# Prompt attention with two output banks in PSUM used in turn, and two in place of three banks for transposed probabilities

## The reference

```python
def block(q0):                       # 128 queries
    s = einsum('bqghd,bngd->bqghn', qc, ck) * SCALE      # compressed keys
    p_c = masked_softmax(s, ...)
    o_c = einsum('bqghn,bngd->bqghd', p_c, cv)
    ...
    p_s = masked_softmax(s, kpos <= pos)                 # selected blocks of 64 keys
    o_s = einsum('bqghm,bqgmd->bqghd', p_s, v_s)
    ...
    p_w = masked_softmax(s, wm)                          # window of 512 keys
    o_w = einsum('bqghk,bkgd->bqghd', p_w, v_w)
    return g[..., 0:1] * o_c + g[..., 1:2] * o_s + g[..., 2:3] * o_w
```

## Time and profile before

| | us |
|---|---|
| median of 3 runs | 2075.46 |
| lowest, highest | 2073.04, 2078.39 |
| profiled execution, device time | 2073.38 |
| its span, first to last instruction | 2071.7 |
| prompt attention, first scores' preparation to last drain | 446.4 to 807.4 |
| mean granted clock of TensorE | 0.927 |

### The profile page before, as it was taken

How to read it: one execution, slowest core, us unless ns; L and a number is a source line. 1 busy time by engine, 2 the same in 40 slices (tenths; PEclk the granted TensorE clock), 3 DMA queues, 4 the chain that set the end, 5 groups by cost and what they waited for, 6 DMA issues and landing times. The chain is left out here.

```text
span 2071.7 us, 26793 instructions
## 1 busy us (share of the span) xinstructions
PE 1848.6 (89%) x9832; PEld 1586.5 (77%) x9832; DVE 1039.9 (50%) x1928; ACT 837.6 (40%) x1702; POOL 185.4 (9%) x334
## 2 busy tenths in 40 slices
PE   5996995979888997949969996999999999999997
PEld 4896873668677775738847885999998999989996
DVE  3532244857677875445434343544445544464444
ACT  4310222536566665232126442433334433343443
POOL 0001202114333321010000000000000000000000
PEclk8998796977889998969979998999999999999998
DMA  5513604400000002133012110333334333344431
GB/s 183 199 45 74 152 4 132 124 9 1 1 1 1 1 1 76 56 136 124 1 61 93 51 61 11 133 122 123 134 139 161 124 122 121 121 159 156 153 130 66
DMA packets 110649, 184.56 MB, mean 89 GB/s; under 512 B 19248, under 2 KB 80112, under 8 KB 110471
## 3 DMA queue, kind: packets, MB, share of 16 engines
q1 hardware_dynamic: 90495, 156.32, 22.0%
q0 software_dynamic: 8080, 25.26, 3.7%
q10 hardware_dynamic: 11968, 1.58, 0.6%
HBM read 174.64 MB, written 12.73 MB: 90 GB/s over the span
## 5 line engine op out<-in xcount | busy, mean ns | idle before, releaser
L2406 DVE TENSOR_TENSOR mlp_dn_lo<-top_w_out_raw,mlp_dn_hi 128x1024 fp32r<-128x1024 f32 x96 | 117.6, 1225 | 299.5 <-ACT mlp_dn_hi L2329 299.5
L2246 PE MATMUL mlp_psU<-mlp_xT_hi,mlp_up_hi 128*128 128x384 f32 (+1 forms) x768 | 253.9, 331 | 5.3 <-DVE mlp_up_lo L2400 5.3
L2246 PE MATMUL mlp_psU<-mlp_xT_lo,mlp_up_hi 128*128 128x384 f32 (+1 forms) x768 | 252.1, 328 | 0.0
L2246 PE MATMUL mlp_psU<-mlp_xT_hi,mlp_up_lo 128*128 128x384 f32 (+1 forms) x768 | 252.0, 328 | 0.0
L2329 ACT CAST mlp_dn_hi<-top_w_out_raw 128x1024 fp32r<-128x1024 f32 x96 | 100.6, 1048 | 267.4 <-PE mlp_acc L2268 187.4
L2268 PE MATMUL mlp_acc<-mlp_dn_hi,mlp_h_hi 128*128 128x512 f32 x512 | 199.4, 389 | 0.0
L2268 PE MATMUL mlp_acc<-mlp_dn_hi,mlp_h_lo 128*128 128x512 f32 x512 | 199.2, 389 | 0.0
L2268 PE MATMUL mlp_acc<-mlp_dn_lo,mlp_h_hi 128*128 128x512 f32 x512 | 199.2, 389 | 0.0
L2246 PEld LDWEIGHTS mlp_psU<-mlp_xT_hi,mlp_up_hi 128*128 128x128 f32 x768 | 145.0, 189 | 9.4 <-issue 3.3
L2246 PEld LDWEIGHTS mlp_psU<-mlp_xT_lo,mlp_up_hi 128*128 128x128 f32 x768 | 145.1, 189 | 3.1
L2246 PEld LDWEIGHTS mlp_psU<-mlp_xT_hi,mlp_up_lo 128*128 128x128 f32 x768 | 145.0, 189 | 0.0
(11 more groups left out here) (399 smaller groups left out, 3974.0 us busy)
## 6 DMA issues: line engine op xcount, KB each, us to landing
top_w_out_raw<-in_w_up SPq DMA_DIRECT2D x48, 1024.0 KB
top_w_out_raw<-in_w_down SPq DMA_DIRECT2D x48, 1024.0 KB
cross_mem<-in_cache_mem_kv SPq DMA_DIRECT2D x8, 1024.0 KB, 4.9
qkv_w_raw<-in_w_in SPq DMA_DIRECT2D x8, 652.0 KB, 5.9
mem_w_raw<-in_w_mkv SPq DMA_DIRECT2D x8, 512.0 KB, 4.9
cmp_raw<-in_cache_cmp_kv SPq DMA_DIRECT2D x32, 128.0 KB
cmp_raw<-in_cache_cmp_kv POOLq DMA_DIRECT2D x32, 128.0 KB, 6.6
smp_sel<-in_cache_sel_kv SPq DMA_DIRECT2D x32, 128.0 KB
```

Source lines behind the costliest of these rows:

```text
L2246: m = nc.tensor.matmul(psU[n % 2][:, 0:w], a[:, u % 2, c, :], b[:, g % 2, c, 0:w], start=(c == 0 and n_pass == 0), stop=(c == KC - 1 and n ...
L2406: nc.vector.tensor_tensor(dn_lo[:, u % 2], dn_raw[:, k, a, :], dn_hi[:, u % 2].bitcast(F32), ALU.subtract).then_inc(s_dl, 1)
```

## The change

The output of a unit gets two banks, taken in turn by u % 2; the first product of unit u waits for the drain of unit u-2 in place of u-1. The transposed probabilities (and the prep steps' transposes) get two banks in place of three, so a transposing step waits for the drain of the one two before it in place of three. The number of banks stays eight. No instruction is added or removed.

```diff
-        psT = [ph.ps(f"psT{k}", [P, 4, P]) for k in range(3)]
-        psO = ph.ps("psO", [P, 4, P])
+        psT = [ph.ps(f"psT{k}", [P, 4, P]) for k in range(2)]
+        psO = [ph.ps(f"psO{k}", [P, 4, P]) for k in range(2)]
...
                     pe.wait_ge(s_th, n + 1)
-                    if arg == 0 and u:
-                        pe.wait_ge(s_od, u)
-                    out = psO[:, :, :].rearrange("p a b -> p (a b)")
+                    if arg == 0 and u >= 2:
+                        pe.wait_ge(s_od, u - 1)
+                    out = psO[u % 2][:, :, :].rearrange("p a b -> p (a b)")
...
-                        halves = psO[:, :, :].rearrange("p (m e) t -> p e m t", e=2)
+                        halves = psO[u % 2][:, :, :].rearrange("p (m e) t -> p e m t", e=2)
```

## The result

| | before | after |
|---|---|---|
| median of the runs, us | 2075.19 (4 runs) | 2094.57 (4 runs) |
| lowest, highest | 2073.04, 2078.39 | 2091.33, 2097.20 |
| profiled execution, device time | 2073.38 | 2095.39 |
| its span | 2071.7 | 2093.7 |
| end of the last drain (start and length of the last L1431) | 807.4 | 829.4 |

The ratio of the times is 1.0091 [1.0075, 1.0108]: the change costs 19.4 us on the medians, where the sum said 22.5.

A forecast was written before the change was run, and what follows sets the result against it. No engine is full; an order of waits sets the attention stage's time, and the kernel follows it. Passes 11 to 14, 6 to 10, 1 to 5, 15 and 16: 11 + 3 + 5.5 + 3 = 22.5 us, so 2098; range 2075.46 + 8 to 2118.

The forecast's parts named there:

- Part 1, gain 0: Two output banks: a unit's first product already finds the drain of the unit before finished; gain 0.
- the 2.2 us of room: Pass 11: time from the output's last add to the next unit's first product, 2.2 us, tightest of 15.
- Passes 11 to 14, 11 us: 10 heads with a preparation step lose 1.1 us each, as transposes wait for later drains: 11.0 us, ends 8 and 16.
- The walk through the second head of pass 12: Head with blocks a, b, c and a preparation step: c starts 1.4 us later, next head's a 1.1 us later.
- The clock: Rival: more waits lower the clock from 617.4 us on to 0.82, 15 us more, 2113; chance 0.16.
- Passes 1 to 5, 5.5 us: Largest transpose-wait shortfall of each pass counted as lost, 1.0 to 1.8 us in four passes: 5.5 us, ends 0 and 9.
- Passes 6 to 10, 3 us: 12 heads with a preparation step lose 0.25 us each, existing holes covering most: 3 us, ends 0 and 13.
- Passes 15 and 16, 3 us: Pass 15 loses 0.9 in its first head; pass 16 has blocks every 1.02 us: together 3, ends 1 and 5.
- Plain heads at nothing: Heads without preparation step: c's 0.2 us delay falls into TensorE's 0.33 us hole before the window scores; cost 0 to 0.1.
- Hidden waits: Rival: ScalarE's and VectorE's chain sets heads with a preparation step, hiding TensorE's delay; 3 us, 2078.5; chance 0.11.
- all shortfalls exposed: Rival: every transpose wait counts in full, the high ends together, 43 us, 2118; chance 0.06.
- The output bank: Rival: output drains did bind, so 15 come free, 19 us; about 2070 with the hidden case; chance 0.03.

The follow-up runs named there:

- the kernel after it: Kernel before, with scaling ahead of the last block and, in heads without prep step, VectorE's window maximum ahead of the first block's drain: 0.9979, 2069.34 us.

## Why the prediction was right, and where not

**Part 1, gain 0: right.** With one output bank the time is the same, 1.0084 beside 1.0093, with intervals that largely overlap. No row of the waits has a product that waits for L1431, and the 2.2 us of room were the right thing to read. The order of the work gave the overlap already, and the bank came out of another rotation, at a loss of 0.9%. The Trainium skill (Perfetto Trace Analysis, section on optimizing Tensor performance, matmuls) asks for a rotation of independent matmul groups through different PSUM banks; this case's runs show no gain from it for the output.

**Passes 11 to 14, 11 us: right mechanism, term too small; 13.8.** The walk through the second head of pass 12 holds up to the selection scores: b and c start 0.06 after the drains (0.05 taken), and these scores come 4.60 us after a (4.63 worked out). The window scores follow 0.87 us later, not 1.03, so the period is 6.69 where the walk gave 6.87 (6.6 to 6.9 was forecast), and this head costs 0.91, not 1.1. Pass 12 has two prep heads and stays at 1.00: it takes 26.15 where it took 24.27, 0.94 each. Pass 11 has three; in the trace without a low clock it takes 27.56 where it took 24.25, 1.10 each. At this rate, 1.04, ten would give 10.4, close to the forecast. Another 3.4 us came on top: in one trace of two a fall of the clock in pass 11, and in passes 13 and 14 more than the rate in both.

**The clock, in part.** The stretch went from 1.00 (0.98 in the second trace of the kernel before) to 0.95, not to 0.82, and its price, as the mean of two traces, is at most the 3.4 us just named, not 15. One pair of waits shows a price. In pass 11 the second and third blocks of the first head wait 0.96 and 1.48 us in the first trace of the changed kernel, 0.96 and 1.49 in the second. TensorE, first trace:

```profile
670.26 0.66 PE L1289 MATMUL att_psT<-top_ident,att_prob 128*128 128x128 f32 x4 [0.96 <-DVE att_pT_lo L1422]
672.39 0.66 PE L1289 MATMUL att_psT<-top_ident,att_prob 128*128 128x128 f32 x4 [1.48 <-DVE att_k_lo L1373]
...
673.54 0.63 PE L1253 MATMUL att_psA<-att_k_hi,att_qS 128*128 128x512 f32 x1
```

Second trace, the same three:

```profile
671.17 0.66 PE L1289 MATMUL att_psT<-top_ident,att_prob 128*128 128x128 f32 x4 [0.96 <-DVE att_pT_lo L1422]
673.32 0.66 PE L1289 MATMUL att_psT<-top_ident,att_prob 128*128 128x128 f32 x4 [1.49 <-DVE att_k_lo L1373]
674.28 0.40 PE L1253 MATMUL att_psA<-att_k_hi,att_qS 128*128 128x512 f32 x1
```

The 512-column matmul takes 0.63 in the first and 0.40 in the second. Windows of the first trace (columns as above, the clock third from the end) put the low stretch right behind the two waits:

```profile
668.00:672.00 4.00, 1.83 (x13) 1.28 (x12) 3.62 (x7) 3.10 (x7) 0.08 (x1) 1.00 0.00 0
672.00:676.00 4.00, 3.61 (x15) 3.09 (x15) 2.64 (x6) 1.36 (x5) 1.23 (x2) 0.64 0.00 0
```

The whole pass takes 29.13 with it and 27.56 without: 1.57 us for one spell of half clock (29.14 with such a spell in the kernel with one output bank). The first trace has two more such spells in these passes, around 728 and 758 us, each behind two waits for the prep steps' and blocks' drains (0.96 and 1.66 us, 1.09 and 1.07); both are in all three traces of kernels with this rotation (the change twice, and one output bank). What these two cost was not separated. At 1.1 per prep head, passes 13 and 14 are left with 0.9 and 1.4 us, but here the prediction's "10 prep heads of this kind" fails: with 13 blocks in four heads the prep step stands elsewhere among them. In the second head of each pass one long wait takes the place of two short ones:

```profile
736.65 0.66 PE L1289 MATMUL att_psT<-top_ident,att_prob 128*128 128x128 f32 x4 [1.78 <-DVE att_qS L1379]
...
766.85 0.66 PE L1289 MATMUL att_psT<-top_ident,att_prob 128*128 128x128 f32 x4 [1.94 <-DVE att_qS L1379]
```

In the third head of pass 13 no block waits for a prep step. From a to the next a, the prep heads of pass 13 go from 4.34, 5.99 and 6.20 us to 7.66, 7.26 and 5.97, those of pass 14 from 4.09 and 6.42 to 6.86 and 8.07 (first traces), so neither 1.1 each nor 6.6 to 6.9 describes them. How much of the surplus is the clock and how much these waits stays open.

The rule of the Trainium skill (TensorE: Matmul & The Clock Gate, "A second HAM failure mode: psum-queue depth-cycling") that micro-idles from cycling PSUM banks make the clock oscillate agrees with this trace, 0.95 with three spells.

A rotation of two banks isn't the only source of such spells. The second trace of the kernel before, with three banks, has one in pass 10 and one in pass 14, which cost 0.34 and 0.15 us by the length of the passes. The kernel with the scaling put ahead, also with three, has one in pass 11, which takes 25.47 us where the kernel after it, without a spell, takes 24.37, and one in pass 13 without a loss (25.95 and 26.23). That the waits bring the spells rests on their place and on their return in three traces; it isn't shown. With a bank of their own for the prep steps these waits are gone, and that trace has no spell in passes 11 to 14; but the first trace of the kernel before has none there either, and the second has one, so a single trace decides nothing here.

**Passes 1 to 5, 5.5 us: too large; 2.1.** The delays are there. In pass 5 block 1 (the counterpart of the earlier trace rows) now waits for the key prep's drain, which ends at 534.32 + 0.68 = 535.00:

```profile
534.32 0.68 DVE L1373 TENSOR_TENSOR att_k_lo<-att_psT,att_k_hi 128x512 fp32r<-128x512 f32 x1
...
535.06 1.12 PE L1289 MATMUL att_psT<-top_ident,att_prob 128*128 128x128 f32 x4 [0.77 <-DVE att_k_lo L1373]
```

What failed is the step that took the largest shortfall of a pass as lost. Pass by pass the change is +0.9, -1.0, +1.5, -0.2 and +0.8 us between the means. Passes 1 and 3 lost 0.9 and 1.5, in both traces alike, where 1.1 and 1.0 were worked out. Pass 4, with the largest shortfall (1.8), lost nothing. Pass 5 takes 22.19 us in the first trace; in the second its block 1 waits 1.07 us for the same drain, and the pass takes 20.67 (20.74 and 20.56 before). So the delay alone didn't lengthen pass 5; where it disappears stays open.

**Passes 6 to 10, 3 us: within its bounds, not to be settled.** The sums are 118.8 and 115.7 before, 116.7 and 120.3 after; two traces of the same kernel differ by more than the term. The clock of 542.4 to 617.4 was 0.82 in the earlier trace rows and 0.95 after, 0.89 in the second trace after.

**Passes 15 and 16, 3 us: 1.5.** Pass 16 is as worked out: 2.1 us more (19.7 for 17.6). Two blocks of it, the counterpart of the earlier trace rows:

```profile
820.11 0.66 PE L1289 MATMUL att_psT<-top_ident,att_prob 128*128 128x128 f32 x4
820.28 0.69 DVE L1422 TENSOR_TENSOR att_pT_lo<-att_psT,att_pT_hi 128x512 fp32r<-128x512 f32 x1 [0.22 <-ACT att_pT_hi L1345]
...
822.17 0.65 PE L1289 MATMUL att_psT<-top_ident,att_prob 128*128 128x128 f32 x4
```

Two fills take 2.06 us, 1.03 each (1.02 predicted). Pass 15 was to lose 0.9 and is 0.6 shorter (29.8 for 30.4), in every trace with two banks for the blocks; why stays open.

**Plain heads at nothing: right number, wrong reason in part.** c's 0.2 us do fall into the hole. But the period is not ScalarE's and VectorE's alone: TensorE's window scores and a are in it. A delay of a, or of the window scores, would have counted in full, and in prep heads it did, once the hole of 0.28 us was gone.

**The rivals.** Hidden waits fell with the 13.8 us of passes 11 to 14; all shortfalls exposed (43 in all) fell with passes 4 and 5 and with the total. The output bank fell with the kernel that leaves it out; its forecast time doesn't come out of its terms (2075.46 less 19, plus the 3 of the hidden case, is 2059, not 2070), and nothing else was built on it. The number of waiting weight loads was 59 (39 + 14 + 3, and 3 of prep steps), of 50 to 80.

The stage lost 18.6 us and the medians 19.4, 3 to 4 below the sum. That the total is so close is in part luck, as the terms erred in both directions: 2.8 too little in passes 11 to 14, 6.7 too much in the three other groups (4.8 measured of 11.5).

## What to carry to other kernels

Before a buffer is given from one rotation to another, read in the timeline when each bank is refilled and when its last reader ended: the output had 2.2 us of room, the transposes none, and the trade cost 0.9%. A rotation shared by two streams can be as slow as the later drain of the two: the prep steps' lagging drain cost the blocks most of the time, and a bank of their own for the prep steps took back three quarters of the loss. A walk through one pass holds for passes of the same arrangement: two passes of one block more had other waits. An engine that waits for another isn't thereby out of the loop that sets the period; follow the loop once round until it closes before a delay is called hidden.

## What the runs showed of the hardware

- The same waits (0.96 and 1.48 us, then 0.96 and 1.49) were followed by half clock in one execution and by full clock in the other. One such spell cost 1.57 us there, and 0.15 and 0.34 us in two passes of the kernel before.
- The start of the stage moved from 451.1 to 455.3 us between two executions of the unchanged kernel, a fifth of the effect studied here: single traces are compared by the length of a stage, not by points of time.
